# State-space scan of a hybrid decoder trunk: its transposes, decays and products issued between the sixteen gate tiles, and the decay sums broadcast from bf16 parts

## The chip, the cores and the metric

One core of a Trainium2 chip runs the whole program. The metric is the device time in microseconds (us). The engines are TensorE (matrix products, PE in the profile; PEld are its weight loads), VectorE (DVE), ScalarE (ACT), GpSimd (POOL) and SyncE (SP, which issues the loads). PSUM has eight banks, into which TensorE writes and from which VectorE and ScalarE read.

## What is computed

Two layers over 256 tokens of width 1024, all in fp32. The change lies in the token mixer of the first layer, a Mamba-2 block with 32 heads of 64 in 4 groups, state size 128 and chunks of 128 tokens (so two chunks). Cut to that:

```python
z, xbc, dt = jnp.split(h @ w_in, [SSD_D_INNER, SSD_D_INNER + SSD_CONV_DIM], axis=-1)
xbc = jax.nn.silu(causal_depthwise_conv(xbc, conv_w, conv_b))
xs, bm, cm = jnp.split(xbc, [SSD_D_INNER, SSD_D_INNER + g * n], axis=-1)
dt = jax.nn.softplus((dt + dt_bias).astype(jnp.float32)).reshape(bsz, s, g, hg)
...
def step(state, inp):
    acs = jnp.cumsum(dtc * a, axis=1)
    seg = acs[:, :, None] - acs[:, None, :]
    decay = jnp.exp(jnp.where(mask, seg, -jnp.inf))
    cb = jnp.einsum('blgn,bsgn->blsg', cc, bc)
    w = cb[..., None] * decay * dtc[:, None]
    y = jnp.einsum('blsgh,bsghp->blghp', w, xc)
    y = y + jnp.einsum('blgn,bghpn->blghp', cc, state) * jnp.exp(acs)[..., None]
    tail = jnp.exp(acs[:, -1:] - acs) * dtc
    state = (state * jnp.exp(acs[:, -1])[..., None, None]
             + jnp.einsum('bsgh,bsgn,bsghp->bghpn', tail, bc, xc))
    return state, y
...
y = y.astype(h.dtype).reshape(bsz, s, SSD_D_INNER) * jax.nn.silu(z)
y = rmsnorm(y.reshape(bsz, s, g, SSD_NORM_GROUP), norm_g.reshape(g, SSD_NORM_GROUP))
return y.reshape(bsz, s, SSD_D_INNER) @ w_out
```

After it come an expert block with product keys (PEER), an HGRN2 mixer, and a second PEER block. They are not changed.

## The kernel before

Every engine has its own program, written out in order; semaphores tie them together. `dve.wait_ge(seg_mm, q + 1)` makes VectorE wait until the semaphore `seg_mm` has reached that count, and nothing behind it on VectorE runs before.

**The streams.** All weights come in tiles of 1024x128, in the order of `STREAM`: 24 tiles `ssd_in` (x, B and C of the mixer), 16 tiles `ssd_z` (the gates z), 16 tiles `ssd_out`, and so on. SyncE loads a tile into one of four buffers `raw`. ScalarE rounds it to `whi` (`hi`, L435), and `wlo` is the rest `raw - whi`: VectorE makes it for `ssd_in`, GpSimd for `ssd_z` and `ssd_out` (`los`, L403 on). TensorE needs both: `split` (L699) multiplies a tile in 24 products (whi with hhi, whi with hlo, wlo with hhi, over 8 pieces) into one of the banks 0 to 3 (`project`, L721). ScalarE copies the result out (`copy_to`, L460) before that bank is used again; the rounding of tile t + 2 stands in its program ahead of the copy of tile t, and waits until tile t - 2 has been multiplied.

**The conv.** Each `ssd_in` tile goes into `pad` and `xc`; VectorE adds three more taps (`conv_tap`, L1107, twelve instructions per four tiles), and ScalarE applies silu to four tiles at once (`conv_silu`, L497). Between the taps VectorE works out the step sizes `dt` and the cumulated sums `acs` on 32 rows of `small` (`dt_input`, `dt_log`, `dt_sums`, `dt_tail`). The taps of the last four tiles come when VectorE has nothing else in its program.

**The scan's steps.** They are issued after all 16 gate tiles: (1) five small transposes give per-token scalars, copied to `tok5`; (2) 32 transposes (L782) bring x to token-major form in eight groups over seven banks, and VectorE multiplies them by dt and the tail into `xdt` and `xtail` (L1201); (3) four transposes of B, eight products of B and C, masked into `cbm`; (4) for each pair of heads q, TensorE copies two rows of `acs` to all partitions, as fp32 products of a column of the identity on 32 rows with `acs` (L805); VectorE subtracts the token's own sum and clamps at 0 (L1218), into `decay`; ScalarE exponentiates `cexp` and, each fourth q, two pieces of `decay` (L537, L542); a bank is used again after both have read it; (5) the products for the state (L813) go to banks 4 to 7, and ScalarE copies them to `state`; (6) VectorE weights `decay` and `cexp`, three instructions of 128x1024 for each of the four groups (L1228, L1231); (7) `y_tiles` (L820) makes the outputs in banks 0 to 7, VectorE adds the skip (L1239) and multiplies by the silu of the gates (L1248), which needs `z_act`; (8) squares, means, roots and norms of the groups, then the `ssd_out` tiles (`accumulate`, L848).

`decay` lies in the same memory as `pad`: it can be written once the taps are done.

Of the kernel before, what the change touches and what calls it, by code (L numbers as in the profile page):

```python
# [24 lines left out]
ALU = mybir.AluOpType  # L25
# [68 lines left out]
def trunk(nc, x_t, par, con, w_dt, weights, sub_keys, out_t):  # L94
# [11 lines left out]
    with ctx:  # L106
# [141 lines left out]

        sq = work(0, 2048, KC)
# [184 lines left out]
        def _(act):  # L434
# [90 lines left out]
            stream("ssd_z", copy_to(col), 0, 1)  # L525
            conv_silu(4)
            stream("ssd_z", copy_to(col), 1, 2)
            conv_silu(5)
            stream("ssd_z", copy_to(col), 2)
            act.wait_ge(evac, SSD_TILES)  # L530
            nc.scalar.activation(zs, zs, ACT.Silu).then_inc(z_act, 1)

            for q in range(HEADS // 2):

                act.wait_ge(seg_v, q + 1)
                src = bank[q % 4][:, :].rearrange("p (h t) -> p h t", h=2)[:, :, P:T]
# [161 lines left out]
        def _(pe):  # L698
# [22 lines left out]
            def project(name, a=0, b=None):  # L721

                def body(i):
                    for r in range(RAW):
# [5 lines left out]
                        split(bank[r][:, 0:T], r, True, True, name if first else None).then_inc(mm_done, 1)  # L730
                b = COUNT[name] // RAW if b is None else b
# [33 lines left out]
            project("ssd_z")  # L765

            pe.wait_ge(dt_v, 4)
# [6 lines left out]
            pe.wait_ge(conv_act, CONV // 4)  # L774
            pe.wait_ge(evac, SSD_TILES)
            for n in range(8):
                c, q = divmod(n, 4)
                b = (0, 1, 2, 3, 5, 6, 7, 0)[n]
                if n == 7:
                    pe.wait_ge(xt_v, 1)  # L780
                for m in range(4):
                    ins = nc.tensor.transpose(bank[b][:, P * m:P * (m + 1)],  # L782
                                              xc[:, 4 * q + m, c * P:(c + 1) * P], ident[:, :])
                ins.then_inc(xt_mm, 1)

            pe.wait_ge(tok_v, 1)
# [808 lines left out]
```

## Time and profile before

| | before |
|---|---|
| median of 3 runs | 2275.22 us (2274.92 to 2276.9) |
| the profiled execution | 2277.54 us |
| its span, first to last instruction | 2275.7 us |
| TensorE busy / mean granted clock | 2154.3 us (95%) / 0.976 |
| VectorE busy | 1129.8 us (50%) |
| ScalarE busy | 1073.5 us (47%) |
| GpSimd busy | 1264.8 us (56%) |

The durations below are from the profiled execution, and times of the trace count from the start of its span. "x32" is a number of instructions that the view merged into a row, with their joint length before it; what stands in brackets is how long the engine was idle ahead of the row, and the instruction whose end ended that. `big` is the name of one large buffer, in which most of the tiles named above lie. A granted clock of 1.00 is 2.4 GHz, 0.50 is 1.2 GHz.

### The profile page before, as it was taken

The page shows a single profiled execution, that of the slowest core. Times are in us where ns is not written, and L with a number is a line of the kernel's source. Part 1 is how long each engine was busy: PE and PEld are TensorE (multiplying, and loading weights), DVE is VectorE, ACT ScalarE, POOL GpSimd, SP SyncE. Part 2 cuts the span into 40 slices and gives each one's busy share as a digit, 9 for nine tenths or more (in the row PEclk, how much of TensorE's full clock was granted, in tenths as well). Part 3 has the DMA queues.
Part 4 walks back from the last instruction along what each step waited for, and adds up shares of the span by engine and source line. Part 5 has one row for each costly group of instructions (what it writes and reads, how often), then busy time and mean ns, then how long its engine had stood idle before and what let it go on. Part 6 is the DMA issues. An engine that isn't in the chain of part 4 may idle for free.

```text
span 2275.7 us, 42335 instructions
## 1 busy us (share of the span) xinstructions
PE 2154.3 (95%) x14562; PEld 1980.2 (87%) x14562; DVE 1129.8 (50%) x1857; ACT 1073.5 (47%) x1559; POOL 1264.8 (56%) x624
## 2 busy tenths in 40 slices
PE   6998899999999999999988978999999999999998
PEld 5996899999999888888878968999999988888886
DVE  5847409990002964444435651699300098444444
ACT  4643345445444444555545434544454444555453
POOL 0250668898885045555547525799888702555552
PEclk9997999999999999999999989999999999999999
DMA  4540444555563056666534313455556403565563
GB/s 147 172 133 19 149 148 157 174 167 192 187 199 106 1 176 193 193 193 194 193 119 150 110 56 130 158 167 169 182 196 200 166 1 114 192 193 193 193 193 102
DMA packets 97708, 345.66 MB, mean 152 GB/s; under 512 B 10480, under 2 KB 14064, under 8 KB 97264
## 3 DMA queue, kind: packets, MB, share of 16 engines
q1 hardware_dynamic: 94512, 340.67, 45.4%
q10 hardware_dynamic: 3136, 4.19, 0.7%
q8 instruction: 36, 0.59, 0.1%
q14 instruction: 24, 0.20, 0.0%
HBM read 341.68 MB, written 3.15 MB: 152 GB/s over the span
## 4 chain that ended last, share of the span: by engine, by line
PE 52%; issue 25%; POOL 21%; DVE 1%; POOLq 0%; ACT 0%; DVEq 0%; ACTq 0%
PE bank L1010 31%; POOL wlo L394 20%; PE bank L708 14%; PE bank L989 5%; PE bank L977 2%; PE bank L748 0%; DVE big L1044 0%; POOLq L398 0%; POOLq L393 0%; DVE rstd L1042 0%; DVE big L1514 0%; ACT hhi L667 0%; POOL hlo L428 0%; POOL big L412 0%; POOL big L411 0%
## 5 line engine op out<-in xcount | busy, mean ns | idle before, releaser
L394 POOL TENSOR_TENSOR wlo<-raw,whi 128x1024 fp32r<-128x1024 f32 x360 | 907.9, 2530 | 470.6 <-ACT whi L440 469.3
L708 PE MATMUL bank<-hhi,whi 128*128 128x256 f32 x3072 | 880.8, 287 | 61.1 <-DVE hlo L1054 26.4
L708 PE MATMUL bank<-hlo,whi 128*128 128x256 f32 x3072 | 876.0, 285 | 0.0
L708 PE MATMUL bank<-hhi,wlo 128*128 128x256 f32 x3072 | 875.7, 285 | 0.0
L440 ACT ACTIVATE whi<-raw 128x1024 fp32r<-128x1024 f32 x640 | 675.6, 1056 | 385.8 <-PE bank L1010 330.4
L708 PEld LDWEIGHTS bank<-hhi,whi 128*128 128x128 f32 x3072 | 597.0, 194 | 68.8 <-issue 49.9
L428 POOL TENSOR_TENSOR hlo<-big,hhi 128x256 fp32r<-128x256 f32 x256 | 352.9, 1380 | 515.5 <-ACT hhi L672 515.5
L708 PEld LDWEIGHTS bank<-hlo,whi 128*128 128x128 f32 x3072 | 596.9, 194 | 0.1
L708 PEld LDWEIGHTS bank<-hhi,wlo 128*128 128x128 f32 x3072 | 596.6, 194 | 0.0
L1510 DVE TENSOR_TENSOR wlo<-raw,whi 128x1024 fp32r<-128x1024 f32 x256 | 316.7, 1238 | 367.1 <-ACT whi L440 366.9
L1010 PE MATMUL bank<-whi,hhi 128*128 128x512 f32 x1024 | 315.4, 389 | 3.4 <-POOL hlo L428 3.4
L1010 PE MATMUL bank<-wlo,hhi 128*128 128x512 f32 x1024 | 315.3, 389 | 0.0
L1010 PE MATMUL bank<-whi,hlo 128*128 128x512 f32 x1024 | 315.1, 389 | 0.0
L644 ACT ACTIVATE big<-bank 128x256 f32 x256 | 98.4, 385 | 395.2 <-PE bank L708 394.8
L1010 PEld LDWEIGHTS bank<-whi,hhi 128*128 128x128 f32 x1024 | 192.0, 188 | 44.0 <-issue 4.4
L1010 PEld LDWEIGHTS bank<-wlo,hhi 128*128 128x128 f32 x1024 | 192.2, 188 | 40.0
L1010 PEld LDWEIGHTS bank<-whi,hlo 128*128 128x128 f32 x1024 | 192.2, 188 | 40.0
L1496 DVE SCALAR_TENSOR_TENSOR raw<-bank,gate_t 128x512 f32<-128x512 f32 x128 | 88.3, 691 | 192.9 <-PE bank L977 188.3
L989 PEld LDWEIGHTS bank<-raw,hhi 128*128 128x128 f32 x1024 | 134.1, 191 | 20.1 <-ACT hhi L667 2.0
L989 PE MATMUL bank<-raw,hhi 128*128 128x128 f32 x1024 | 135.1, 275 | 1.1 <-ACT hhi L667 1.1
L667 ACT ACTIVATE hhi<-bank 128x512 fp32r<-128x512 f32 x128 | 76.2, 597 | 92.4 <-PE bank L977 92.4
L672 ACT ACTIVATE hhi<-big 128x256 fp32r (+1 forms) x256 | 102.1, 399 | 4.6 <-DVE big L1487 4.6
(220 smaller groups left out, 1368.8 us busy)
## 6 DMA issues: line engine op xcount, KB each, us to landing
raw<-w_u SPq DMA_DIRECT2D x256, 512.0 KB, 3.4
raw<-w_v SPq DMA_DIRECT2D x256, 512.0 KB, 4.3
raw<-w_ssd_in SPq DMA_DIRECT2D x40, 512.0 KB, 3.4
raw<-w_q SPq DMA_DIRECT2D x32, 512.0 KB, 3.5
raw<-w_hgrn_in SPq DMA_DIRECT2D x32, 512.0 KB, 3.5
raw<-w_ssd_out SPq DMA_DIRECT2D x16, 512.0 KB, 3.4
raw<-w_hgrn_out SPq DMA_DIRECT2D x8, 512.0 KB, 3.5
big<-keys SPq DMA_DIRECT2D x2, 1024.0 KB, 5.5
```

What stands on the lines that cost most here:

```text
L394: nc.gpsimd.tensor_tensor(wlo[:, r, :, :], raw[:, r, :, :], whi[:, r, :, :].bitcast(F32), ALU.subtract).then_inc(lo_pool, 1)
L428: nc.gpsimd.tensor_tensor(hlo[:, r, :], big[:, bass.ds(j, 1), :].rearrange("p a b -> p (a b)"), hhi[:, r, :].bitcast(F32), ALU.subtract).t ...
L440: nc.scalar.activation(whi[:, r, :, :], raw[:, r, :, :], ACT.Copy).then_inc(hi_done, 1)
L644: nc.scalar.activation(col(t), bank[r][:, 0:T], ACT.Gelu).then_inc(evac, 1)
L667: nc.scalar.activation(oha[n % 4], bank[4 + n % 2][:, :].rearrange("p (n k) -> p n k", n=4), ACT.Relu).then_inc(oha_done, 1)
L672: nc.scalar.activation(hhi[:, r, :], col(j), ACT.Copy).then_inc(chi, 1)
L708: ins = nc.tensor.matmul(out, w[:, r, k, :], h[:, k, :], start=start and n == 0, stop=stop and n == 3 * KC - 1, **kw)
L977: nc.tensor.matmul(bank[4 + 2 * c + n % 2][:, :], feat_rows[:, 2 * c + n // 32, n % 32 // 4, :], signs[:, 4 * (n % 4):4 * (n % 4) + 4, :], ...
L989: ins = nc.tensor.matmul(bank[n % 4][:, P * t:P * (t + 1)], oha[n % 4][:, t, :].bitcast(F32), ohb[n % 4][:, t, :], start=True, stop=True)
L1010: ins = nc.tensor.matmul(bank[4 + 2 * b + e][:, :], c[:, r, tok], w[:, r, 4 * e:4 * e + 4, :], start=False, stop=True, skip_group_check=True)
L1496: nc.vector.scalar_tensor_tensor(out=ohb[n % 4], in0=bank[6 + n % 2][:, :].rearrange("p (n k) -> p n k", n=4), scalar=0.0, in1=gate_t[:, 4 ...
L1510: nc.vector.tensor_tensor(wlo[:, r, :, :], raw[:, r, :, :], whi[:, r, :, :].bitcast(F32), ALU.subtract).then_inc(lo_dve, 1)
```

## The change

- The sums `acs` are split on VectorE into three bf16 parts, which lie on 96 rows (`dt_parts`), with a bf16 selector of 96 rows (`dt_sel`). `dt_split` follows `dt_tail`, ahead of the `ssd_in` tile 17's subtraction. A broadcast is then one bf16 product over 96 rows in place of an fp32 product over 32.
- TensorE issues the steps (1) to (4) between single gate tiles: the token scalars and x groups around tiles 2 to 5, B ahead of tile 6, the B and C products ahead of tile 7, and two head pairs ahead of each of tiles 8 to 15. The x groups use banks 5, 6, 7 in turn, the sums banks 7, 4, 5, 6, since 0 to 3 are the gate tiles'.
- ScalarE writes out the sixteen gate tiles one by one; the last two silus of the conv come after tiles 1 and 4, and after tiles 8 to 15 two exponentials for `cexp` each, with those of `decay`. The silu of the gates moves from ahead of the exponentials to behind the copies of the states, with a table load of its own.
- The state products follow the last gate tile and wait for all segments. VectorE weights groups 0 and 1 within the segments (after q = 9 and q = 13), the other two after them.

```diff
+        dt_parts = small[0:96, 0, 0:P].bitcast(BF16)
+        dt_sel = small[0:96, 1, 0:HEADS // 2].bitcast(BF16)
+        dt_mid = small[0:HEADS, 1, P:T].bitcast(BF16)
+        XT_BANK = (5, 6, 7, 5, 6, 7, 5, 6)
+        SEG_BANK = (7, 4, 5, 6)
...
-            stream("ssd_z", copy_to(col), 0, 1)
-            conv_silu(4)
-            stream("ssd_z", copy_to(col), 1, 2)
-            conv_silu(5)
-            stream("ssd_z", copy_to(col), 2)
-            act.wait_ge(evac, SSD_TILES)
-            nc.scalar.activation(zs, zs, ACT.Silu).then_inc(z_act, 1)
...
+            evacuate = copy_to(lambda t: big[:, t, :])
+            for t in range(XT):
+                g = FIRST["ssd_z"] + t
+                hi(g + 2, (t + 2) % RAW)
+                evacuate(t, t % RAW, g)
+                if t == 1:
+                    conv_silu(4)
+                elif t == 4:
+                    conv_silu(5)
+                    nc.scalar.preload_act_table_set("natural_log_exp_and_others")
+                elif t >= 8:
+                    decays(2 * t - 16)
+                    decays(2 * t - 15)
             act.wait_ge(st_mm, 1)
             for g in range(GROUPS):
                 nc.scalar.activation(state[:, g, :], bank[4 + g][:, :], ACT.Copy).then_inc(st_a, 1)
+            nc.scalar.preload_act_table(ACT.Silu)
+            act.wait_ge(evac, SSD_TILES)
+            nc.scalar.activation(zs, zs, ACT.Silu).then_inc(z_act, 1)
             nc.scalar.preload_act_table(ACT.Sqrt)
...
+            def gate_tile(t):
+                project("ssd_z", t // RAW, rs=[t % RAW])
+
+            def x_tokens(n):
+                c, q = divmod(n, 4)
+                if n >= 3:
+                    pe.wait_ge(xt_v, n - 2)
+                for m in range(4):
+                    ins = nc.tensor.transpose(bank[XT_BANK[n]][:, P * m:P * (m + 1)],
+                                              xc[:, 4 * q + m, c * P:(c + 1) * P], ident[:, :])
+                ins.then_inc(xt_mm, 1)
+
+            def segment(q):
+                if q >= 4:
+                    pe.wait_ge(seg_v, q - 3)
+                    pe.wait_ge(seg_a, q - 3)
+                for e in range(2):
+                    h = 2 * q + e
+                    ins = nc.tensor.matmul(bank[SEG_BANK[q % 4]][:, e * T:(e + 1) * T],
+                                           dt_sel[:, h:h + 1].to_broadcast([96, P]), dt_parts, start=True, stop=True)
+                ins.then_inc(seg_mm, 1)
+            gate_tile(0)
+            gate_tile(1)
             pe.wait_ge(dt_v, 4)
...
+            pe.wait_ge(conv_act, 4)
+            for n in range(4):
+                x_tokens(2 * n)
+                x_tokens(2 * n + 1)
+                gate_tile(n + 2)
+
+            pe.wait_ge(conv_act, 6)
             pe.wait_ge(tok_v, 1)
             for g in range(GROUPS):
                 ins = nc.tensor.transpose(bank[4][:, P * g:P * (g + 1)], b_t[:, g, 0:P], ident[:, :])
             ins.then_inc(bt_mm, 1)
+            gate_tile(6)
             for c in range(NB):
-                pe.wait_ge(xt_v, 5 + c)
+                pe.wait_ge(xt_v, 7 + c)
...
+            gate_tile(7)
+            pe.wait_ge(dt_v, 5)
             pe.wait_ge(bt_v, 1)
             pe.wait_ge(cb_v, 2)
+            for n in range(8):
+                segment(2 * n)
+                segment(2 * n + 1)
+                gate_tile(n + 8)
+
+            pe.wait_ge(seg_v, 16)
+            pe.wait_ge(seg_a, 16)
             for g in range(GROUPS):
                 ins = nc.tensor.matmul(bank[4 + g][:, :], btok[:, g, :], xtail[:, 512 * g:512 * (g + 1)],
                                        start=True, stop=True)
             ins.then_inc(st_mm, 1)
...
+            def dt_split():
+
+                for a in range(0, 96, HEADS):
+                    nc.vector.tensor_copy(dt_sel[a:a + HEADS, :], ident[a:a + HEADS, a:a + HEADS])
+                step(nc.vector.tensor_copy(dt_parts[0:HEADS], acs))
+                step(nc.vector.tensor_tensor(w, acs, dt_parts[0:HEADS], ALU.subtract))
+                step(nc.vector.tensor_copy(dt_mid, w))
+                step(nc.vector.tensor_tensor(w, w, dt_mid, ALU.subtract))
+                nc.vector.tensor_copy(dt_parts[HEADS:2 * HEADS], dt_mid)
+                step(nc.vector.tensor_copy(dt_parts[2 * HEADS:3 * HEADS], w))
+                nc.vector.tensor_copy(dt_mid[:, 0:1], dt_mid[:, 0:1]).then_inc(dt_v, 1)
...
                     dt_tail()
+                    dt_split()
                     forget_bounds()
...
+            dve.wait_ge(cb_v, 2)
+            for q in range(HEADS // 2):
+                dve.wait_ge(seg_mm, q + 1)
+                for e in range(2):
+                    h = 2 * q + e
+                    for c in range(NB):
+                        ins = nc.vector.tensor_scalar(decay[:, c, h, :],
+                                                      bank[SEG_BANK[q % 4]][:, e * T + c * P:e * T + (c + 1) * P],
+                                                      tok5[:, 2 + c, h:h + 1], 0.0, ALU.subtract, ALU.min)
+                ins.then_inc(seg_v, 1)
+                if q in (9, 13):
+                    weigh(q // 4 - 2)
+            for g in range(2, GROUPS):
+                weigh(g)
```

`weigh(g)` holds the three weighting products of group g, as in step (6). `decays(q)` holds the exponentials of step (4).

## Rows read from the trace of the kernel before

**Rows 1.** ScalarE's timeline: start, length, line, what, count, idle before it

```profile
103.48 0.38 ACT L493 ACTIVATE big<-bank 128x256 f32<-128x256 f32 x1 [1.09 <-PE bank L708]
...
149.66 0.38 ACT L463 ACTIVATE big<-bank 128x256 f32 x1 [1.54 <-PE bank L708]
150.07 3.62 ACT L531 ACTIVATE big<-big 128x4096 f32<-128x4096 f32 x1
...
189.64 2.07 ACT L545 ACTIVATE big<-bank 128x512 f32<-128x512 f32 x4 [3.14 <-PE bank L813]
191.72 1.28 ACT L546 ACT_TABLE_LOAD   x1
```

**Rows 2.** TensorE's timeline behind the last gate tile

```profile
150.19 3.69 PE L782 MATMUL bank<-ident,big 128*128 128x128 f32 x32 [0.24 <-ACT big L463]
...
158.43 24.60 PE L805 MATMUL bank<-small,ident 32*128 32x256 f32 x64
182.96 6.64 PE L813 MATMUL bank<-big 128*128 128x512 f32 x8
191.96 0.29 PE L831 MATMUL bank<-big 128*64 128x128 f32 x1 [2.36 <-ACT big L545]
...
201.88 1.99 PE L844 MATMUL bank<-big,ones 128*128 128x256 f32 x8
```

**Rows 3.** VectorE's timeline in the same stretch

```profile
150.92 7.26 DVE L1201 TENSOR_TENSOR big<-bank,big 128x512 f32<-128x512 f32 x12 [0.61 <-PE bank L782]
...
159.90 4.21 DVE L1218 TENSOR_SCALAR big<-bank,big 128x128 f32<-128x128 f32 x16
...
184.11 2.35 DVE L1228 TENSOR_TENSOR big<-big 128x1024 f32<-128x1024 f32 x2
...
203.38 1.65 DVE L1239 SCALAR_TENSOR_TENSOR big<-big,pars,bank 128x256 f32<-128x256 f32 x4
205.07 1.23 DVE L1248 TENSOR_TENSOR big<-big 128x1024 f32<-128x1024 f32 x1
```

**Rows 4.** TensorE by stretch: its length, busy us, granted clock, share of DMA, GB/s

```profile
150.00:154.00 4.00, 3.81 (x35) 1.00 0.58 205
162.00:188.00 26.00, 26.00 (x56) 0.50 0.00 0
217.00:223.00 6.00, 5.44 (x22) 0.50 0.00 0
1237.00:1240.00 3.00, 3.00 (x14) 0.50 0.54 171
```

**Rows 5.** VectorE's timeline in the input tiles

```profile
44.96 0.41 DVE L1125 TENSOR_TENSOR small<-small 32x256 f32<-32x256 f32 x1
...
80.92 1.22 DVE L1104 TENSOR_TENSOR wlo<-raw,whi 128x1024 fp32r<-128x1024 f32 x1
```

**Rows 6.** Timeline of VectorE and GpSimd at the last conv taps

```profile
98.60 1.66 DVE L1114 SCALAR_TENSOR_TENSOR big<-big,pars 128x256 f32<-128x256 f32 x4
...
104.36 18.29 DVE L1114 SCALAR_TENSOR_TENSOR big<-big,pars 128x256 f32<-128x256 f32 x12 [4.10 <-ACT big L494]
...
106.29 10.06 POOL L394 TENSOR_TENSOR wlo<-raw,whi 128x1024 fp32r<-128x1024 f32 x4 [1.40 <-ACT whi L440]
```

**Rows 7.** Timeline of VectorE and GpSimd in the HGRN stage

```profile
1247.66 2.48 POOL L394 TENSOR_TENSOR wlo<-raw,whi 128x1024 fp32r<-128x1024 f32 x1 [1.80 <-ACT whi L440]
...
1247.81 3.41 DVE L1341 TENSOR_TENSOR big<-big 128x1024 f32<-128x1024 f32 x1
...
1253.42 2.62 DVE L1350 COPY_PREDICATED big<-ident,bank 128x512 f32<-128x512 uint32 x4
```

**Rows 8.** TensorE's waits in 205:220 and 1225:1240: total us, times, longest

```profile
PE bank L741 <- DVE big L1248: 7.9, 1, 7.9
...
PE bank L708 <- POOL wlo L394: 4.6, 1, 4.6
```

**Rows 9.** Line 1282 of the HGRN stage: duration ns min/median/max, first and last start

```profile
L1282 DVE TENSOR_SCALAR big<-big,lbt x8: 402/1448/2524, 1217.1 to 1227.8; 128x256 f32<-128x256 f32 x8
```

More of the change, by code:

```diff
@@ L524, in _, with decays @@
             conv_silu(3)
-            stream("ssd_z", copy_to(col), 0, 1)
-            conv_silu(4)
-            stream("ssd_z", copy_to(col), 1, 2)
-            conv_silu(5)
-            stream("ssd_z", copy_to(col), 2)
-            act.wait_ge(evac, SSD_TILES)
-            nc.scalar.activation(zs, zs, ACT.Silu).then_inc(z_act, 1)
-            for q in range(HEADS // 2):
+            def decays(q):
                 act.wait_ge(seg_v, q + 1)
-                src = bank[q % 4][:, :].rearrange("p (h t) -> p h t", h=2)[:, :, P:T]
+                src = bank[SEG_BANK[q % 4]][:, :].rearrange("p (h t) -> p h t", h=2)[:, :, P:T]
                 nc.scalar.activation(cexp[:, 2 * q:2 * q + 2, :], src, ACT.Exp).then_inc(seg_a, 1)
@@ L719, in tile_ready, with project, body @@
                     pe.wait_ge(lo_pool, POOL_LO[name] + RAW * i + r + 1)
-            def project(name, a=0, b=None):
-                def body(i):
-                    for r in range(RAW):
+            def project(name, a=0, b=None, rs=None):
+                def body(i, rs=range(RAW)):
+                    for r in rs:
                         tile_ready(name, i, r)
@@ L730, in body @@
                         split(bank[r][:, 0:T], r, True, True, name if first else None).then_inc(mm_done, 1)
+                if rs is not None:
+                    body(a, rs)
+                    return
                 b = COUNT[name] // RAW if b is None else b
@@ L764, in _ @@
             project("ssd_in", 1)
-            project("ssd_z")
+            def gate_tile(t):
[19 more added lines that the diff above has]
+            gate_tile(1)
             pe.wait_ge(dt_v, 4)
@@ L772, in _ @@
             ins.then_inc(tok_mm, 1)
[L774 to L784, printed above, removed]
+            pe.wait_ge(conv_act, 4)
[4 more added lines that the diff above has]
+            pe.wait_ge(conv_act, 6)
             pe.wait_ge(tok_v, 1)
@@ L796, in _ @@
                 ins.then_inc(cb_mm, 1)
-            pe.wait_ge(xt_v, 8)
-            for q in range(HEADS // 2):
-                if q >= 4:
-                    pe.wait_ge(seg_v, q - 3)
-                    pe.wait_ge(seg_a, q - 3)
-                for e in range(2):
-                    h = 2 * q + e
-                    ins = nc.tensor.matmul(bank[q % 4][:, e * T:(e + 1) * T],
-                                           ident[0:HEADS, h:h + 1].to_broadcast([HEADS, P]),
-                                           small[0:HEADS, 7, :], start=True, stop=True)
-                ins.then_inc(seg_mm, 1)
+            gate_tile(7)
+            pe.wait_ge(dt_v, 5)
             pe.wait_ge(bt_v, 1)
             pe.wait_ge(cb_v, 2)
+            for n in range(8):
[4 more added lines that the diff above has]
+            pe.wait_ge(seg_a, 16)
             for g in range(GROUPS):
@@ L815, in _ @@
             ins.then_inc(st_mm, 1)
-            pe.wait_ge(seg_v, 16)
-            pe.wait_ge(seg_a, 16)
+            pe.wait_ge(evac, SSD_TILES)
             pe.wait_ge(st_a, GROUPS)
@@ L1194, in _ @@
                 c, q = divmod(n, 4)
-                b = (0, 1, 2, 3, 5, 6, 7, 0)[n]
+                b = XT_BANK[n]
                 dve.wait_ge(xt_mm, n + 1)
@@ L1211, in _, with weigh @@
                     .then_inc(cb_v, 1)
-            for q in range(HEADS // 2):
-                dve.wait_ge(seg_mm, q + 1)
-                for e in range(2):
-                    h = 2 * q + e
-                    for c in range(NB):
-                        ins = nc.vector.tensor_scalar(decay[:, c, h, :],
-                                                      bank[q % 4][:, e * T + c * P:e * T + (c + 1) * P],
-                                                      tok5[:, 2 + c, h:h + 1], 0.0, ALU.subtract, ALU.min)
-                ins.then_inc(seg_v, 1)
-            dve.wait_ge(cb_v, 2)
-            for g in range(GROUPS):
+            def weigh(g):
                 hs = slice(8 * g, 8 * g + 8)
```

## The prediction

> **What bounds the kernel now.** I began with the timeline of TensorE after the last gate tile and compared it with those of ScalarE, VectorE and GpSimd. Up to 149.7 us TensorE is the bound. The sixteen gate tiles leave it at an even pace: ScalarE begins to copy the last input tile at 103.48 and the last gate tile at 149.66, so one tile takes 46.18 / 16 = 2.89 us, or 0.12 us for each of its 24 products [rows 1]. Meanwhile VectorE is idle for most of the time. Then comes a chain in which the engines take turns. TensorE issues the x transposes (3.7 us for 32, 0.115 each), the B and C products, the 64 broadcast instructions (24.6 us), and the state products (6.6 us), and it starts the outputs only at 191.96 [rows 2]. VectorE makes the token-major tiles (12 in 7.3 us), then the decays; from 184.11 it runs the twelve weighting products and the output sums without a gap, and the last gating product of the first three groups starts at 205.07 [rows 3]. This is my **mark**: from there to the first tile of the out-projection the code and its order are the same in both kernels, so that the movement of the mark is the movement of the whole. The broadcasts take so long because they are fp32 on 32 rows and because the granted clock is at half, 1.2 GHz, in all of 162 to 188 us although TensorE is busy throughout [rows 4].
>
> **The splitting of the sums (added).** Three small copies, then six instructions on 32x256 and a last one on one column, one waiting for the other. A 32x256 subtraction costs 0.41 us [rows 5], the copies less; I take 2.5 us, between 1.2 (copies at half the price) and 3.5. It stands ahead of the subtraction for input tile 17, which begins at 80.92 and lasts 1.22 [rows 5]. Tile 17 leaves TensorE six tiles before the last one, at 103.48 - 6 x 2.89 = 86.2, and so starts at 83.3 [rows 1], and 1.2 us of the 2.5 are hidden. **Cost 1.3 us** (0 to 2.3). GpSimd works on nothing then.
>
> **Work of TensorE moved between the gate tiles.** It is no longer after them but it lengthens their stretch: 37 transposes and 4 for B at 0.115 (4.7 us), the B and C products (16 instructions of the same size and 0.115 each, 1.8, with 0.2 for handing over) and 32 bf16 products of 256 columns. The nearest row for these is the gate tile's own product of 256 columns, 0.12 us: 0.48 for the four of a pair of segments, 3.9 us in all instead of 24.6. The bound above is 0.9 a pair. With nothing waiting, the gate stretch would thus grow by some 10.5 us, and the 24.6, the 3.7 and the 2.0 would be gone behind it. There are two stalls, though.
>
> **Stall 1: the conv taps.** The x groups have three banks where they had seven, so x_tokens(3) waits for VectorE's first xdt product, and that stands behind the twelve last conv taps. Alone, four taps take 1.66 us; beside GpSimd, twelve take 18.3 (104.36 to 122.65), while GpSimd makes four wlo tiles in 10.06 [rows 6]. If the first four went at their own speed, the other eight took 2.1 each, nearly a GpSimd instruction's 2.5: both want the same path, and they take turns. Walk, in times of the profile before: gate tiles 0 and 1 end at 109.2; the transposes of the token scalars and two x groups take 1.3; gate tile 2 ends at 113.3; x_tokens(3) is reached at 113.7. ScalarE rounds tile 5 at 113.6 to 114.6 and then has to wait for gate tile 3, so that GpSimd runs out of tiles at 117.2. The taps then go at full speed and end at 118.3 rather than 122.65. With the copy of the token scalars (0.4) and two products (1.2) TensorE goes on at **119.9, a stall of 6.2 us**. No edit hides it; it would be gone if the taps went alone.
>
> **The walk on.** x_tokens(3) and tile 3 to 123.2, two more and tile 4 to 126.9, the last two and tile 5 to 130.7, B and tile 6 to 134.1, products and tile 7 to 139.0; GpSimd's and ScalarE's part of each of these tiles is ready. Then eight rounds of 0.48 + 2.88 = 3.36. VectorE needs 16 x 0.26 = 4.2 us for four segments [rows 3], thus 2.1 a round, and keeps up. At the fifth round it reaches q = 9 at 154.8 and turns to weigh(0), three products of 128x1024 from SBUF. The row for this is in the HGRN stage: a product of the same size took 3.41 beside a GpSimd subtraction that had begun just before, and four copies whose source is PSUM ran unhindered in 2.62 [rows 7], while two such products alone took 2.35 [rows 3]. So weigh(0) costs 1.2 + 3.4 + 1.2 = 5.8, to 160.4; q = 10 to 13 are done at 164.6. TensorE has 14 and 15 issued at 163.1, since its banks have just come free, and ends the last gate tile at 166.0. VectorE runs weigh(1) first, with one block again, to 170.3, and the last two segments to 172.3.
>
> **Stall 2: the state products.** They now wait for all sixteen segments: 172.7, **6.7 us after the last gate tile**. In the row of before they took 6.64 at half clock [rows 2], at full clock half of that. ScalarE copies the states in 2.07 and only then loads a table (1.28, as at 191.72) and runs the silu of the gates, 3.62 [rows 1]. Before, that silu lay at 150.07, beside VectorE's work; now it is late. VectorE's weigh(2) and weigh(3), 6.8 us, lie beside the state products. With the state products at half: 172.7 + 6.6 + 2.1 = 181.4. Two output tiles at half clock are 5.0 (six took 9.9 at mixed clock, 191.96 to 201.88 [rows 2]); 186.4 + 0.9 for VectorE = 187.3, and the silu ends at 186.3, just before. From there 1.14 + 1.66 + 1.14 + 1.66 = 5.6 to the mark: 192.9.
>
> **The clock.** After an idle time of 7.9 us TensorE worked at half clock from 217.56 until 223, and after one of 4.6 us in 1237 to 1240 [rows 4, 8]. Stall 1 lies between them (6.2), so I take 2.3 us for work at half clock after it, between 1.7 and 2.9. Stall 2 is priced above.
>
> **Sum.** 192.9 + 1.3 + 2.3 = 196.5 against 205.07: **8.6 us gained**. The profiled execution has a span of 2275.7 and took 2277.54 us; that would become 2268.9. It lies 2.3 above the median of the runs, 2275.22, and so the forecast on the median is **2266.6 us**. Its own range is 2262 to 2273, from the bounds of the split (-1.3 to +1.0), the segments (+1.9), the clock (0.6 either way) and one more or one less block of 2.3 us in each weigh.
>
> **Rivals.**
> (a) *The clock holds.* If neither stall takes the clock down, the 2.3 and half of the 6.6 fall away, the output tiles come early enough and the silu binds, at 172.7 + 3.3 + 2.1 + 4.9 = 183.0, and the mark comes at 183.0 + 5.6 + 1.3 = 189.9: gain 15.2, 2260.0 us. For it: both are idle times whose ends only the walk gives. Against: both are longer than the 4.6 us that sufficed. With one drop 2262 to 2264. Chance 0.27 for the two together.
> (b) *The decays take GpSimd's path too.* They are tensor-scalar instructions, and those of the HGRN stage with source and result in SBUF, 402 ns at best, took 1448 in the median beside GpSimd [rows 9]. No row has a PSUM-sourced one beside it; the nearest is the copy from PSUM [rows 7], unhindered, which is why I leave this out of the sum. If it held, each round would give VectorE one decay for the 2.4 us of GpSimd and the rest after it: the last two rounds and GpSimd's tiles slip, 8.4 us in the walk. Gain about 0, 2275.4 us. Chance 0.08. The Trainium skill, "VectorE: DVE Perf Modes", section "Why PSUM operands drop a tier", says that the mode which uses both SBUF read ports is not open to an instruction that reads PSUM. By that rule (b) doesn't happen; no run here has shown it for this instruction.
> (c) *Slower: the clock stays down.* In 162 to 188 us the clock was at half though TensorE was always busy, with 32-row products [rows 4]. If after stall 1 the mixture of transposes, 96-row products and gate tiles kept it down, each gate tile would cost 24 x 0.09 = 2.2 us more (14 products in the 3.00 us at half clock are 0.21 each, instead of 0.12 [rows 4]). The forecast has 2.3 for this, so with five tiles (8.6 + 2.3 = 10.9) nothing is left, and from eight on (8.6 + 2.3 + 4.6 = 15.5) the kernel is slower by more than can be told. For eight tiles, 3 to 10: 10.9 - 17.6 = -6.7, 2281.9 us. Against: three quarters of that work are the same dense products that got the clock back within 5.7 us both times. Chance 0.06. The Trainium skill, "TensorE: Matmul & The Clock Gate", section "Part 4: PE-mode transpose", says transposes don't count as activity that raises the clock. By it (c) would begin with the transposes around tiles 3 to 5; before, the granted clock was full in 150 to 154 us, through the transposes [rows 4].
> (d) *No contention.* If taps and weights ran at their own speed, both stalls would shrink to 0 and 2.3 us: gain 25.8, 2249.4 us. [Rows 6] speak against it. Chance 0.06.
> That the change doesn't do what it says I leave out: the banks and waits written in the diff give the order that I walked.
>
> **How the numbers follow.** Forecast 0.53, (a) 0.27, (b) 0.08, (c) 0.06, (d) 0.06. The range leaves out (b), (c) and (d), 0.20, and holds the forecast's own range and (a) with some room: 2257 to 2273. A measurement of this kernel tells a change of some 0.2%, 4.6 us. Faster by more: the forecast but for its upper edge (0.50), (a) and (d): 0.83. Within: that edge and (b): 0.11. Slower: (c), 0.06.
>
> **What would show it.** Right: ScalarE copies the last gate tile near 170 us, with one gap of some 6 us between gate tiles 2 and 3, GpSimd idle at its end; taps that take 14 us rather than 18; four bf16 products of about 0.12 us between gate tiles; weigh products of 3.4 us among those of 1.2; state products starting some 7 us after the last gate tile, at half clock; the mark near 196.5. Wrong: decays of more than 0.35 us beside GpSimd (b), half clock beyond tile 4 (c), or no gap ahead of tile 3 (d).

## The result and the profile after

The changed kernel took 2265.7 us (median of 5 runs, 2265.18 to 2268.06) beside 2276.9 for the kernel before in the same session (2274.92 to 2278.55). The ratio is 0.995, with a 95% interval of 0.994 to 0.9961. It is faster by 11.2 us where 8.6 were forecast. The 2266.6 us forecast on the median is 0.9 off, but the forecast started from a median of 2275.22, and the kernel before now stood at 2276.9. Much of that closeness is luck: the split of the sums, each of the two weighings and the stretch behind the mark missed by more than 2 us, and they made up for one another.

The page gives the busy times; the timelines of the engines (start, length, line, what, count, idle before it) give the places of the walk. First the page:

```profile
span 2264.6 us, 42191 instructions
...
PE 2129.7 (94%) x14503; PEld 1963.1 (87%) x14530; DVE 1132.4 (50%) x1867; ACT 1073.6 (47%) x1560; POOL 1266.9 (56%) x624
```

ScalarE, which marks the end of each tile by its copy:

```profile
107.06 0.38 ACT L498 ACTIVATE big<-bank 128x256 f32<-128x256 f32 x1 [1.09 <-PE bank L721]
...
117.14 0.38 ACT L468 ACTIVATE big<-bank 128x256 f32<-128x256 f32 x1 [2.03 <-PE bank L721]
...
128.86 0.39 ACT L468 ACTIVATE big<-bank 128x256 f32<-128x256 f32 x1 [10.39 <-PE bank L721]
...
172.19 0.38 ACT L468 ACTIVATE big<-bank 128x256 f32<-128x256 f32 x1 [1.44 <-PE bank L721]
...
183.98 2.06 ACT L555 ACTIVATE big<-bank 128x512 f32<-128x512 f32 x4 [3.89 <-PE bank L842]
186.06 1.28 ACT L556 ACT_TABLE_LOAD   x1
187.35 3.62 ACT L558 ACTIVATE big<-big 128x4096 f32<-128x4096 f32 x1
```

The last input tile comes at 107.06 where it came at 103.48 [rows 1]; gate tile 2 is copied at 117.14 and gate tile 3 only at 128.86: that is stall 1. The last gate tile follows at 172.19. VectorE in the same stretch:

```profile
107.94 13.88 DVE L1142 SCALAR_TENSOR_TENSOR big<-big,pars 128x256 f32<-128x256 f32 x12 [4.10 <-ACT big L499]
...
157.84 2.16 DVE L1270 TENSOR_SCALAR big<-bank,big 128x128 f32<-128x128 f32 x8 [1.17 <-PE bank L799]
159.92 2.35 DVE L1259 TENSOR_TENSOR big<-big 128x1024 f32<-128x1024 f32 x2
162.19 1.22 DVE L1262 TENSOR_TENSOR big<-big 128x1024 f32<-128x1024 f32 x1
163.32 4.22 DVE L1270 TENSOR_SCALAR big<-bank,big 128x128 f32<-128x128 f32 x16
167.46 4.97 DVE L1259 TENSOR_TENSOR big<-big 128x1024 f32<-128x1024 f32 x2
172.35 3.36 DVE L1262 TENSOR_TENSOR big<-big 128x1024 f32<-128x1024 f32 x1
175.64 2.15 DVE L1270 TENSOR_SCALAR big<-bank,big 128x128 f32<-128x128 f32 x8
...
191.08 1.23 DVE L1293 TENSOR_TENSOR big<-big 128x1024 f32<-128x1024 f32 x1 [0.94 <-ACT big L558]
...
196.73 1.22 DVE L1293 TENSOR_TENSOR big<-big 128x1024 f32<-128x1024 f32 x1
```

The last row is the mark: 196.73, forecast 196.5, before 205.07 [rows 3]. The decays take 0.27 us each (8 in 2.16) though GpSimd subtracts from 154.80 to 159.56; the weighting products of group 0 (159.92 to 163.4) run at their own speed, those of group 1 (167.46 to 175.7) don't: three of them take 8.3 us, where those of group 0 took 3.5. What TensorE waited for between 105 and 200 us (total us, times, longest):

```profile
PE bank L842 <- ACT big L534: 6.2, 1, 6.2
PE bank L789 <- DVE big L1242: 5.9, 1, 5.9
PE bank L859 <- issue: 2.2, 1, 2.2
PE bank L721 <- issue: 1.1, 1, 1.1
```

L789 is stall 1 (forecast 6.2), L842 stall 2 (6.7). And TensorE by stretch (length, busy us, granted clock, share of DMA, GB/s):

```profile
87.00:90.00 3.00, 3.00 (x16) 0.50 0.68 216
124.00:127.00 3.00, 3.00 (x16) 0.50 0.05 16
128.00:170.00 42.00, 40.93 (x347) 1.00 0.39 117
...
178.00:182.00 4.00, 3.65 (x5) 0.50 0.00 0
```

The half clock of the second and of the fourth of these was forecast; the first was not: 87 to 90 us, behind the split.

The mark moved by 8.3 us and the span by 11.1. The other 2.7 lie behind the mark, where code and order are the same. The rows for it are those of the 67 us that begin 2.9 us behind each kernel's mark, before and then after:

```profile
208.00:275.00 67.00, 56.40 (x433) 0.90 0.41 139
```

```profile
199.66:266.66 67.00, 54.75 (x437) 0.95 0.44 142
```

The kernel before was at half clock for some 13 us of them and this one for some 7 (an estimate from the granted clocks: twice what is missing to 1.00, times 67).

### The profile page after: what moved, and what is told of

Read it like the earlier page. It is cut to its first block, busy times and chain, and to the rows that moved or that the text cites. A ratio compares the mean times of both kernels' runs of the same rounds, so it can differ in the third digit from the quotient of the medians.

```text
span 2264.6 us, 42191 instructions
## 1 busy us (share of the span) xinstructions
PE 2129.7 (94%) x14503; PEld 1963.1 (87%) x14530; DVE 1132.4 (50%) x1867; ACT 1073.6 (47%) x1560; POOL 1266.9 (56%) x624
## 4 chain that ended last, share of the span: by engine, by line
PE 53%; issue 25%; POOL 21%; DVE 1%; POOLq 0%; ACT 0%; another core or an unknown queue 0%; DVEq 0%; ACTq 0%
PE bank L1038 31%; POOL wlo L399 20%; PE bank L721 14%; PE bank L1017 5%; PE bank L1005 2%; PE bank L764 0%; DVE big L1072 0%; POOLq L403 0%; POOLq L398 0%; DVE rstd L1070 0%; DVE big L1559 0%; ACT hhi L680 0%; POOL hlo L433 0%; POOL big L417 0%; POOL big L416 0%
```

## The experiments

All runs are told by two numbers beside the time: the **mark**, and the mark less the time at which ScalarE copies the last input tile, which takes out what happened ahead of the gate tiles. Before it is 205.07 - 103.48 = 101.59, after 196.73 - 107.06 = 89.67. The medians of the kernel before beside these runs were 2277.2 (first four), 2276.78 (next four) and 2276.26 us (last four). The runs of one kernel spread by up to 5 us. From the mark to the end, the profiled executions of the thirteen kernels in the table are between 0.0 and 2.9 us shorter than that of the kernel before, though code and order are the same there. So the marks tell more than the medians where less than 3 us is at stake.

| | median us | ratio to before (95%) | mark | less the last input tile |
|---|---|---|---|---|
| the change | 2265.7 | 0.995 (0.994 to 0.9961) | 196.73 | 89.67 |
| e1_bf16_only | 2271.44 | 0.9975 (0.9965 to 0.9984) | 202.39 | 93.91 |
| e2_move_only | 2270.21 | 0.9964 (0.9951 to 0.9977) | 199.59 | 95.34 |
| e3_split_late | 2266.85 | 0.9957 (0.9943 to 0.997) | 195.18 | 91.83 |
| e4_weigh1_late | 2258.88 | 0.9918 (0.9903 to 0.9933) | 187.88 | 82.62 |
| e5_no_last_taps | 2258.62 | 0.9921 (0.9906 to 0.9937) | 188.57 | 81.57 |
| e6_warm | 2266.2 | 0.9952 (0.9936 to 0.9967) | 195.31 | 87.75 |
| e7_later_x | 2264.68 | 0.9948 (0.9933 to 0.9963) | 191.69 | 86.49 |
| e8_best | 2262.89 | 0.9942 (0.9929 to 0.9956) | 192.17 | 88.15 |
| e9_later_x_weigh1 | 2259.09 | 0.992 (0.9905 to 0.9935) | 190.61 | 83.48 |
| e10_weigh1_pieces | 2260.9 | 0.9927 (0.9911 to 0.9942) | 188.89 | 82.09 |
| e11_three | 2260.36 | 0.9925 (0.9912 to 0.9939) | 190.57 | 83.50 |
| e12_memset | 2252.95 | 0.9894 (0.9878 to 0.9909) | 182.70 | 75.74 |

**Each half alone.** The bf16 broadcasts in the old place (against the kernel before):

```diff
+            pe.wait_ge(dt_v, 5)
             pe.wait_ge(xt_v, 8)
...
-                                           ident[0:HEADS, h:h + 1].to_broadcast([HEADS, P]),
-                                           small[0:HEADS, 7, :], start=True, stop=True)
+                                           dt_sel[:, h:h + 1].to_broadcast([96, P]), dt_parts, start=True, stop=True)
...
                     dt_tail()
+                    dt_split()
```

> The kernel before with the split and the bf16 broadcasts alone, in their old place behind the gate tiles. The walk's theory: the 24.6 us of broadcasts shrink until VectorE's decays bind (16 x 1.04 = 16.6 us from 159.9, so they end at 176.5 instead of 184.1, -7.6 us), and the split costs the 3.6 us that the last input tile came later in the changed kernel: some 4 us faster than before, mark near 201. Rival 'the cheap broadcast is the whole gain': as fast as the changed kernel, about 10 us faster than before.

Measured: 7.7 us less from the last input tile to the mark, the 7.6 expected, and 5.8 in the median; the rival's 10 didn't come. VectorE's timeline shows what binds when TensorE's broadcasts no longer do, the 64 decays in one piece:

```profile
164.90 16.61 DVE L1234 TENSOR_SCALAR big<-bank,big 128x128 f32<-128x128 f32 x64
```

The move with the old fp32 products of 32 rows (against the changed kernel, whose split is left out):

```diff
-                                           dt_sel[:, h:h + 1].to_broadcast([96, P]), dt_parts, start=True, stop=True)
+                                           ident[0:HEADS, h:h + 1].to_broadcast([HEADS, P]),
+                                           small[0:HEADS, 7, :], start=True, stop=True)
...
-            pe.wait_ge(dt_v, 5)
...
-                    dt_split()
```

> The changed kernel with the fp32 broadcasts over 32 rows and without the split: the move alone. The walk's theory: 16 x 0.85 = 13.6 us at full clock instead of 3.9 between the gate tiles, +9.7, and the split's 3.6 us less: 6 us slower than the changed kernel, 5 faster than before, mark near 203, if the clock stays up between gate tiles. Rival 'the 32-row products pull the clock down wherever they stand': half clock in the eight rounds, some 18 us more, slower than before.

Measured: a clock that stays at full between the gate tiles, and a short stall 2. TensorE by stretch, then its waits:

```profile
126.00:182.00 56.00, 55.29 (x388) 1.00 0.31 96
```

```profile
PE bank L789 <- DVE big L1229: 5.9, 1, 5.9
...
PE bank L842 <- ACT big L534: 1.1, 1, 1.1
```

So the halves gain 7.7 and 6.2 us on the mark alone, 13.9 by their sum, and 11.9 together. Counted from the last input tile, the bf16 form brings the copy of the last gate tile 11.9 us forward (from 181.32 - 104.25 = 77.1 to 172.19 - 107.06 = 65.1), but the mark only 5.7: the state products then wait 6.2 us for VectorE instead of 1.1, and run at half clock. The expectation for e2 (9.7 us more than the changed kernel between the last input tile and the mark) had left that out; 5.7 came.

**The split.** Put behind the taps of the fifth group, where I took VectorE to be free:

```diff
                     dt_tail()
-                    dt_split()
...
                 if i < 4:
                     in_lo(4 * i + 9)
+                if i == 4:
+                    dt_split()
```

> The changed kernel with the split behind the taps of the fifth group, where VectorE was idle for 4.1 us. Theory: all of the 3.6 us by which the last input tile came later (1.8 us of waiting for tile 17 and 1.7 from a stretch at half clock behind it) is the split's place: 3.6 us faster. Rival: the half clock in that stretch is chance and only the 1.8 us go.

Measured: the last input tile came at 103.35 instead of 107.06, 3.7 us earlier. But 2.2 of it were given back by the mark, and the median shows no gain (2266.85 against 2265.7). VectorE's timeline:

```profile
100.05 4.94 DVE L1186 CAST small<-ident 32x32 bf16<-32x32 f32 x3
105.00 0.28 DVE L1187 CAST small<-small 32x256 bf16<-32x256 f32 x1
...
106.52 2.32 DVE L1191 COPY small<-small 32x256 bf16<-32x256 bf16 x1
108.86 2.39 DVE L1192 CAST small<-small 32x256 bf16<-32x256 f32 x1
...
111.35 9.17 DVE L1142 SCALAR_TENSOR_TENSOR big<-big,pars 128x256 f32<-128x256 f32 x12
```

GpSimd makes the first gate tiles' `wlo` from 99.46 to 104.77 and from 106.16 to 111.10, and each copy or cast that meets it lasts as long as one of its instructions; the cast at 105.00, in the gap, takes 0.28. The taps begin at 111.35, 7.1 us after the last input tile is there for them (104.2), and stall 1 grows from 5.9 to 8.3. The Trainium skill, "SBUF — State Buffer", section "Who interferes with whom", says that VectorE's copies and casts, in the modes that use two ports, contend with GpSimd for a pair of ports that the two engines share, and that whoever issues first keeps it for the whole instruction. These rows agree: 2.3 and 2.4 us where alone it is 0.22 and 0.28. In which mode they ran no row shows.

**The weights of group 1.** Rows of the profile after showed them in two blocks, ahead of the last two segments' decays:

```diff
-                if q in (9, 13):
-                    weigh(q // 4 - 2)
-            for g in range(2, GROUPS):
+                if q == 9:
+                    weigh(0)
+            for g in range(1, GROUPS):
                 weigh(g)
```

> The changed kernel with weigh(1) behind the last segment instead of ahead of the last two. Theory: the second stall is made by weigh(1), which took 8.3 us beside GpSimd ahead of segments 14 and 15; without it the last decay ends at about 169.5 instead of 177.7, the state products follow the last gate tile at once and at full clock, and the silu of the gates ends near 183: mark near 188.5, 8 us faster. Rival 'VectorE is the bound': weigh(1) is only moved, its 3.4 us come back behind the last segment, and 2 to 5 us are gained.

Measured: 7.05 us less from the last input tile to the mark, 6.8 in the median against the changed kernel's. The gap ahead of the state products is down from 6.2 to 1.1 us (TensorE's timeline), and they run at full clock, 3.67 us instead of 5.59:

```profile
171.42 3.67 PE L842 MATMUL bank<-big 128*128 128x512 f32 x8 [1.12 <-ACT big L534]
```

It is GpSimd that now waits, some ten microseconds in which nobody needs its tiles of `ssd_out` (its timeline; two instructions of 2.5 us):

```profile
166.96 14.91 POOL L399 TENSOR_TENSOR wlo<-raw,whi 128x1024 fp32r<-128x1024 f32 x2 [0.81 <-ACT whi L445]
```

The expectation's rival, 2 to 5 us, fell. Of all kernels here that compute the whole, this one has the lowest median, with e9's within the spread: 18 us (0.8%) below the kernel before.

This run also settles a question that e3 left open. Its split stands where the changed kernel has it, and TensorE waits there for the same 1.78 us, but the clock stays at full (TensorE's timeline and stretch in e4, then the same stretch in the changed kernel):

```profile
84.82 0.38 PE L721 MATMUL bank<-hhi,whi 128*128 128x256 f32 x1 [1.78 <-ACT big L499]
```

```profile
86.00:90.00 4.00, 4.00 (x36) 1.00 0.69 227
```

```profile
86.00:90.00 4.00, 4.00 (x23) 0.58 0.72 208
```

Its last input tile comes at 105.26. From the input tile copied at 77.62 (77.56 before, 77.32 in e4) to the last one it is 25.9 us before, 29.4 in the changed kernel and 27.9 in e4. So the place of the split costs 2.0 us by the wait alone, and 1.5 more when the clock falls behind it. Of the ten profiled executions with the split in this place eight have the fall, and e4 and e7 don't.

**Stall 1.** Twelve taps left out, so that the four tiles of C get one tap of four:

```diff
-                act.wait_ge(conv_step, 12 * i + 12)
+                if i == 5:
+                    act.wait_ge(evac, 24)
+                act.wait_ge(conv_step, 12 * min(i, 4) + 12)
...
-            for i in range(CONV // 4):
+            for i in range(CONV // 4 - 1):
```

> The changed kernel without the last twelve conv taps: the last four conv tiles (C) get one tap instead of four, so that part of the computation is left out. Theory: the first stall is made by these taps beside GpSimd; without them TensorE does not wait in front of x_tokens(3) (5.9 us in the changed kernel) and keeps its clock (1.6 us at gate tile 3): last gate tile 7.5 us earlier, mark near 189. Rival 'TensorE would wait for the wlo tiles of GpSimd anyway': the gap stays between gate tiles 2 and 3, or moves to tiles 4 to 6, and 3 us at most are gained.

Measured: no wait at x_tokens(3), the last gate tile at 164.15 instead of 172.19, the mark 8.1 us earlier. Stall 1 with its clock is thus worth 8 us: from the copy of gate tile 2 to that of gate tile 3 it is 11.72 us in the changed kernel (128.86 - 117.14) and 3.74 here (120.81 - 117.07), which is 5.9 of waiting and 2.1 for the half clock behind it.

**The clock in stall 2.** Products of zeros in bf16 keep TensorE busy:

```diff
+            pe.wait_ge(evac, SSD_TILES)
+            for _ in range(26):
+                nc.tensor.matmul(bank[0][:, :], zero[:, 0:P], zero[:, :], start=True, stop=True)
             pe.wait_ge(seg_v, 16)
```

> The changed kernel with 26 bf16 products of zeros between the last gate tile and the wait for the last segments, into a bank that is free. Nothing waits for them. Theory: the state products took 6.1 us because the clock fell in the second stall; with the stall filled they take 3.3, and the silu of the gates, which binds, comes 2.8 us earlier: mark near 194, 3 us faster. Rival 'the clock there costs nothing': another wait, such as VectorE's weighting, is just as late, and less than 1 us is gained.

Measured, TensorE by stretch:

```profile
172.00:184.00 12.00, 9.81 (x39) 1.00 0.29 87
184.00:200.00 16.00, 15.17 (x208) 1.00 0.01 2
203.00:214.00 11.00, 5.80 (x27) 0.53 0.07 10
```

The state products take 3.67 us and the mark comes 1.9 us earlier: that was the price of half clock in stall 2. The median, 2266.2, isn't lower: behind the mark TensorE worked at half clock from 208.2 to 213.3 in this run, where the changed kernel did from 209.6 to 212.8, and once more from 241 to 244.

**Taking stall 1 away by order.** The x groups 3 to 7 go behind gate tiles 6 to 8, B and C behind them, and the segments in threes from tile 11 on:

```diff
-            for n in range(4):
-                x_tokens(2 * n)
-                x_tokens(2 * n + 1)
-                gate_tile(n + 2)
-
+            for n in range(3):
+                x_tokens(n)
+            for t in range(2, 7):
+                gate_tile(t)
+            x_tokens(3)
+            x_tokens(4)
+            gate_tile(7)
...
-            for n in range(8):
-                segment(2 * n)
-                segment(2 * n + 1)
-                gate_tile(n + 8)
+            for t in range(11, 16):
+                for q in SEGS[t]:
+                    segment(q)
+                gate_tile(t)
```

> The changed kernel with the x groups 3 to 7 moved behind gate tiles 6 to 8 (the conv's last silu behind tile 7), B ahead of tile 9, the B and C products ahead of tile 10, the segments in threes ahead of tiles 11 to 14, two ahead of tile 15 and two behind it. Theory: TensorE no longer waits for the taps, which may now take 18 us beside GpSimd, so the last gate tile ends 6 us earlier, near 166; weigh(1) still holds up the last segments, which end near 173.5, and 4 to 5 us are gained. Rival 'VectorE binds': its work after the taps starts 5 us later, and nothing is gained, or 2 us are lost.

Measured: 3.2 us less from the last input tile to the mark; the wait for the taps is gone, stall 2 (L853 here) has stayed, and a wait of another kind has come (TensorE's waits):

```profile
PE bank L853 <- ACT big L535: 6.0, 1, 6.0
PE bank L802 <- ACT big L535: 4.2, 5, 1.8
```

L802 is `segment`: with three head pairs a round ScalarE's exponentials hold the banks. That, the split late and weigh(1) late together:

> The order of e7_later_x with the split as in e3_split_late and weigh(1) as in e4_weigh1_late. Theory, with each stall's cause gone: last decay near 168, state products straight behind it at full clock, silu to 180, mark near 183: 13 us faster than the changed kernel, 24 faster than before. Rival 'VectorE binds': taps to 122, token-major tiles, decays and weighting follow without a gap, and the mark is near 188 as in e4_weigh1_late: 8 faster than the changed kernel.

Measured: 88.15 from the last input tile to the mark and 2262.89 us. The expectation failed by the split: its casts met GpSimd's subtractions again, and the taps behind it ran from 111.99 to 127.7, so that TensorE waited 3.8 us for the x groups after all. With the split back in its early place (the edits of e7 and e4):

> The order of e7_later_x with weigh(1) behind the last segment, and the split where the changed kernel has it. e8_best had the split beside GpSimd's first wlo tiles of the gates, where it held VectorE for 11 us. Theory: without that the last decay ends near 168, the state products follow at full clock, and the mark comes near 185: 3 us faster than e4_weigh1_late. Rival 'ScalarE binds': TensorE waited 4.2 us for the exponentials in e7_later_x, since rounds of three segments leave ScalarE no room, and that takes back the gain: mark near 188, no faster than e4_weigh1_late.

Measured: 2259.09, the same as e4 alone. TensorE no longer waits for the taps, but 4.2 us for ScalarE in the segments and 2.7 ahead of the state products, and from the last input tile to the mark it is 83.48 against e4's 82.62. That ScalarE took what stall 1 gave back is my reading; no run takes ScalarE's waits away.

**The silu of the gates.** e4 with the silu in four pieces, so that VectorE need not wait for the whole (0.94 us in e4's trace):

```diff
-            nc.scalar.activation(zs, zs, ACT.Silu).then_inc(z_act, 1)
+            for g in range(GROUPS):
+                v = zs[:, 4 * g:4 * g + 4, :]
+                nc.scalar.activation(v, v, ACT.Silu).then_inc(z_act, 1)
...
-                        if n == 1:
-                            dve.wait_ge(z_act, 1)
+                        dve.wait_ge(z_act, n // 2 + 1)
```

> e4_weigh1_late with the silu of the gates in four pieces, one for each group, so that the first gating product waits for one. In e4_weigh1_late VectorE waited 0.94 us for the whole silu. Theory: those 0.9 us, mark near 187. Rival: ScalarE's squares come in behind the pieces and hold up the roots, 0.

Measured: 82.09 against e4's 82.62, where 0.9 less was expected, and a median of 2260.9 against 2258.88. The profiled execution had the half clock behind the split again (last input tile at 106.80, e4's at 105.26). No gain can be told. All three edits (e7, e4 and the pieces):

> e9_later_x_weigh1 and e10_weigh1_pieces together. Theory: mark near 183.5, the sum of the two. Rival 'ScalarE binds in the rounds of three': as e10_weigh1_pieces.

Measured: 2260.36 and a mark like e9's. The three bring nothing beyond weigh(1) late.

**Is it GpSimd's reading?** For the gate tiles GpSimd subtracts one column only and fills the rest of `wlo` with zeros (the low part of the gate weights is left out):

```diff
+                if name == "ssd_z":
+                    nc.gpsimd.tensor_tensor(wlo[:, r, 0, 0:1], raw[:, r, 0, 0:1], whi[:, r, 0, 0:1].bitcast(F32),
+                                            ALU.subtract)
+                    nc.gpsimd.memset(wlo[:, r, :, :].rearrange("p k c -> p (k c)").bitcast(BF16)[:, 2:2 * TILE],
+                                     0.0).then_inc(lo_pool, 1)
+                    return
```

> The changed kernel in which GpSimd, for the sixteen gate tiles, subtracts one column and fills the rest of wlo with zeros instead of subtracting it: the low part of the gates' weights is left out, and GpSimd writes but reads nearly nothing. Theory 'both read through one path': the twelve taps take 5 us as they do alone, although GpSimd works beside them, weigh products take 1.14 throughout, TensorE never waits in front of x_tokens(3), and the mark is near 185. Rival 'any GpSimd instruction holds it': a tap waits for each fill as for each subtraction, some 1.8 us if a fill lasts as long as its 2046 elements make it, and the first stall stays, shorter.

Measured, VectorE's and GpSimd's timelines:

```profile
107.83 5.09 DVE L1148 SCALAR_TENSOR_TENSOR big<-big,pars 128x256 f32<-128x256 f32 x12 [4.10 <-ACT big L505]
...
110.01 1.80 POOL L402 MEMSET wlo<- 128x2046 bf16 x1
```

Twelve taps take 5.09 us beside fills of 1.8 us each, where they took 13.88 beside subtractions. There is no wait at x_tokens(3), the weighting products of groups 0 and 1 take 1.2 us each, stall 2 is 1.9 us, and the mark comes 13.9 us earlier from the last input tile. GpSimd's reading and a part of its time (1.8 us a tile for 2.4) are taken away together here; that VectorE's taps ran unhindered through the fill from 110.01 to 111.8 speaks for the reading. The Trainium skill, "SBUF — State Buffer", section "Who interferes with whom", says that a VectorE instruction with two SBUF inputs contends with a GpSimd instruction that reads SBUF, and not with one that only writes it: the rows agree.

## Why the prediction was right, and where it was not

**The split: the term that was mis-sized.** Forecast 1.3 us, measured 3.6 (107.06 against 103.48), and outside the range given for it (0 to 2.3). The steps themselves took 2.7 us, forecast 2.5. The cover of 1.2 us was about 1.0: TensorE ran out of input tiles for 1.8 us. What the step left out was the clock. VectorE's timeline, and TensorE's:

```profile
79.73 0.53 DVE L1186 CAST small<-ident 32x32 bf16<-32x32 f32 x3
...
82.35 0.14 DVE L1193 COPY small<-small 32x1 bf16<-32x1 bf16 x1
...
83.66 1.23 DVE L1132 TENSOR_TENSOR wlo<-raw,whi 128x1024 fp32r<-128x1024 f32 x1
```

```profile
85.12 0.38 PE L721 MATMUL bank<-hhi,whi 128*128 128x256 f32 x1 [1.78 <-ACT big L499]
```

The wait is named for ScalarE's L499; what came last was the subtraction of 83.66, which ends at 84.89. Behind this gap the clock was at half from 86.7 to 90.1. e4, which has the gap and not the fall, shows the two parts: 2.0 us for the gap, inside the range, and 1.5 for the clock, which the term had left out. With the split away from there (e3) the tile comes at 103.35.

**Work moved between the gate tiles: right.** Four bf16 products delay the next gate product by some 0.4 us (0.48 forecast), and a round of the second half takes 3.32 (3.36).

```profile
144.12 0.61 PE L799 MATMUL bank<-small 96*128 96x256 bf16 x4
144.49 0.37 PE L721 MATMUL bank<-hhi,whi 128*128 128x256 f32 x1
```

**Stall 1: right, with its mechanism.** Corrected for the 3.6 us, the walk has the taps end at 121.9; they ended at 121.8, after 13.9 us (14). The wait was 5.9 (6.2), GpSimd had run out of tiles at 121.1 and was idle for 9.1, and the clock after it cost 2.1 (2.3), as worked out at e5. e5 shows that TensorE waits for the taps, and e12 that the taps are slow beside GpSimd's subtractions.

**Last gate tile.** 169.6 by the sum (166.0 + 1.3 + 2.3), 172.19 measured. The difference is 2.3 from the split, -0.3 from the wait of stall 1, -0.2 from the clock, -0.5 from the moved work, and 1.3 that I had not: a pause of 1.1 us ahead of gate tile 14, and what follows from it (four rounds up to tile 11 take 13.30 us, the next four 14.58). The moved work is read from e5: 57.15 us from the last input tile to the last gate tile, less the 46.18 of before and the 1.3, is 9.7, where the walk had 10.1. The profile names no releaser for the pause, but GpSimd's timeline and TensorE's show one:

```profile
161.46 4.18 POOL L399 TENSOR_TENSOR wlo<-raw,whi 128x1024 fp32r<-128x1024 f32 x1 [1.89 <-ACT whi L445]
```

```profile
165.74 0.36 PE L721 MATMUL bank<-hhi,whi 128*128 128x256 f32 x1 [1.07 <-issue]
```

GpSimd's subtraction for this tile lay beside weigh(0) and took 4.18 us instead of 2.4; it ended at 165.64, and TensorE went on 0.1 us later. The walk had let GpSimd slow VectorE down and not VectorE GpSimd.

**Weights and stall 2: the sum right, its parts not.** weigh(0) took 3.5 (5.8), since it began in a pause of GpSimd, which was then held up itself (the 4.18 us above); weigh(1) took 8.3 (5.8), with two blocks. One block less and one more: stall 2 was 6.2 (6.7). The forecast's range had provided for this; it didn't ask whether weigh(1) need stand there at all. e4 shows that it need not, for 7 us. That is the largest thing the prediction passed by: it priced the order as written and took the stall as given.

**State products to the mark.** Half clock came, but only until 182.3: 5.6 us instead of 6.6. The output tiles ran at full clock, so that the silu of the gates, named as the next in line, became the bound (0.94 us ahead of the first L1293). That is 1.0 less for the state products and 1.0 less for the output tiles than forecast. The last 5.6 us were 5.65.

Added up: +2.3 (split) +0.3 (stall 1, its clock, moved work and pause together) -0.5 (stall 2) -1.0 (state products) -1.0 (outputs) = +0.1 against the mark of 196.5; it came at 196.73.

**Behind the mark** I had put nothing; 2.7 us came from there. Over the 67 us that begin 2.9 us behind the mark the granted clock was 0.95 where it had been 0.90. In e6 only 0.8 us came from there, in e11 nothing. Why the clock falls in one execution and not in the other was not tried, and stays open.

**The range.** Its listed bounds add up to more than it says: -1.3 - 0.6 - 4.6 and +1.0 + 1.9 + 0.6 + 4.6 about 2266.6 give 2260 to 2275, not 2262 to 2273. The measurement lies inside either.

**The rivals.** (a) did not come: the clock fell behind both stalls. By e6 the fall cost 1.9 us at stall 2 and by e5 2.1 at stall 1, 4.0 together, where (a) had 15.2 - 8.6 = 6.6. (b) fell: decays of 0.27 us beside GpSimd. (c) fell: full clock from 128 to 170, and by e2 even with the 32-row products between gate tiles. (d) fell; e12 prices it at 13.9 us where (d) had 25.8 - 8.6 = 17.2, with a stall 2 of 1.9 us and a granted clock of 0.82 in 172 to 200 us left.

## What to carry to other kernels

Work moved in between other work takes its place in every in-order queue that it crosses: look for the instruction of it that nobody needs yet (here three weighting products ahead of the last decays), and put it last. Where VectorE and GpSimd both read SBUF, count the meetings one by one, casts and copies of 0.2 us too; each cost up to a whole instruction of the other here, on either engine. A wait of TensorE is to be priced twice, with the stretch at half clock behind it and without: behind 1.8 us of waiting the clock fell in eight executions of ten.

## What was not expected of the hardware

- An idle time of 1.8 us on TensorE (83.34 to 85.12) was followed by half clock from 86.7 to 90.1, although it worked all through the time between. The kernel before, without the idle time, had full clock there; e4 and e7, with the same idle time, had it too.
- fp32 products on 32 rows ran at half clock for 26 us when they stood alone [rows 4], and at full clock for 56 us when gate tiles stood between them (e2).
- A copy of 32x256 bf16 took 2.32 us instead of 0.22, and a cast 2.39 instead of 0.28, beside a GpSimd subtraction (e3). One-input instructions from SBUF to SBUF were held up as those with two inputs were, while those that read one PSUM bank were not (the decays, 0.27 us each).
- GpSimd is held up as well: two subtractions in 14.91 us beside VectorE's row of products (e4), instead of 5, and one in 4.18 instead of 2.4 in the changed kernel, for which TensorE waited 1.1 us.
